# A tile's three products as three passes over its row blocks instead of three products per block

## What is computed

```python
h = _rmsnorm(x, norm_w) * (1.0 + scale[:, None]) + shift[:, None]
proj = h @ w_in
q, k, v, ga, u, gp, z, xbc, dt_raw, gl = jnp.split(proj, ...)
ya = _sink_window_attention(q, k, v, rel_bias, sinks) * silu(ga)
yb = _multiscale_pool(u, pool_w, pool_scale) * silu(gp)
yc = _ssd_branch(z, xbc, dt_raw, ...)
g = sigmoid(gl).reshape(b, s, 3, D_MODEL)
merged = g[:, :, 0] * (ya @ w_pa) + g[:, :, 1] * (yb @ w_pb) + g[:, :, 2] * (yc @ w_pc)
return x + gate[:, None] * (merged @ w_out)
```

## Time and profile before

| | us |
|---|---|
| median of 3 runs (lowest to highest) | 1238.05 (1238.03 to 1238.07) |
| time of the profiled execution | 1237.72 |
| its span, first to last instruction | 1235.8 |
| PE busy in the span | 1155.9 (94%) |
| DVE busy | 602.1 (49%) |
| POOL busy | 532.4 (43%) |
| ACT busy | 513.1 (42%) |
| mean granted TensorE clock | 0.970 |

### The profile page before, as it was taken

The page is one execution under the profiler, slowest core; times in us unless marked ns, Lnnn a source line. Parts: engine busy times, 40 slices in busy tenths (PEclk is TensorE's granted clock), DMA queues, the critical chain, the costliest instruction groups (busy, mean ns, idle before and its releaser), DMA issues.

```text
span 1235.8 us, 14931 instructions
## 1 busy us (share of the span) xinstructions
PE 1155.9 (94%) x5906; PEld 952.6 (77%) x5906; DVE 602.1 (49%) x741; ACT 513.1 (42%) x880; POOL 532.4 (43%) x392
## 2 busy tenths in 40 slices
PE   3289999999999999999989999999999999999996
PEld 2278888887888887788767888888788887778875
DVE  6754115655878633322435222565778754132434
ACT  1234334675543543322334422765454443232332
POOL 1524443444433435554533443453343425454540
PEclk9569999999999999999998999999999999999998
DMA  9824552233444233333223553332534423333321
GB/s 353 281 67 127 182 154 69 73 99 94 127 121 115 74 86 90 104 96 102 86 71 94 143 182 95 86 86 69 147 81 131 112 76 84 103 103 102 86 85 68
DMA packets 211460, 139.18 MB, mean 113 GB/s; under 512 B 11416, under 2 KB 203968, under 8 KB 209344
## 3 DMA queue, kind: packets, MB, share of 16 engines
q1 hardware_dynamic: 209968, 133.52, 37.5%
q10 hardware_dynamic: 1424, 4.72, 1.1%
HBM read 135.08 MB, written 2.62 MB: 111 GB/s over the span
## 4 chain that ended last, share of the span: by engine, by line
PE 82%; DVE 6%; DMA 5%; POOL 3%; ACT 2%; SPq 2%; issue 1%; DVEq 0%; ACTq 0%; POOLq 0%
PE main L462 72%; DMA raw<-in_w_in 4%; PE psC L462 4%; PE psA L462 3%; POOL tmp L421 1%; DVE h_lo L1238 1%; POOL w_lo L429 1%; PE psB L462 1%; DMA icnt<-in_inv_count 1%; DVE xbc L1193 1%; DVE tmp L968 1%; ACT w_hi L725 1%; DVE y_lo L1233 1%; DVE zs L1269 1%; SPq L381 1%
## 5 line engine op out<-in xcount | busy, mean ns | idle before, releaser
L429 POOL TENSOR_TENSOR w_lo<-raw,w_hi 128x512 fp32r<-128x512 f32 x360 | 507.3, 1431 | 644.8 <-ACT w_hi L725 644.8
L462 PE MATMUL main<-h_hi,w_hi 128*128 128x512 f32 x1184 | 473.1, 400 | 14.9 <-DVE h_lo L1010 5.9
L462 PE MATMUL main<-h_hi,w_lo 128*128 128x512 f32 x1184 | 463.4, 391 | 0.0
L462 PE MATMUL main<-h_lo,w_hi 128*128 128x512 f32 x1184 | 463.1, 391 | 0.0
L725 ACT ACTIVATE w_hi<-raw 128x512 fp32r<-128x512 f32 x360 | 208.4, 623 | 383.8 <-PE main L462 303.3
L462 PEld LDWEIGHTS main<-h_hi,w_hi 128*128 128x128 f32 x1184 | 223.8, 189 | 73.3 <-issue 22.0
L462 PEld LDWEIGHTS main<-h_hi,w_lo 128*128 128x128 f32 x1184 | 223.5, 189 | 48.0
L462 PEld LDWEIGHTS main<-h_lo,w_hi 128*128 128x128 f32 x1184 | 224.1, 189 | 46.5 <-issue 1.9
L1227 DVE TENSOR_TENSOR tmp<-main,misc 128x512 f32<-128x512 f32 x32 | 22.1, 691 | 201.9 <-PE main L462 201.9
L1073 DVE SCALAR_TENSOR_TENSOR misc<-main,lcol,misc 128x511 f32<-128x511 f32 (+2 forms) x96 | 71.9, 749 | 65.4 <-ACT misc L725 62.8
L462 PE MATMUL main<-y_hi,w_hi 128*128 128x512 f32 x256 | 101.6, 397 | 1.4 <-DVE y_lo L1233 1.4
(11 more groups left out here) (189 smaller groups left out, 1017.9 us busy)
## 6 DMA issues: line engine op xcount, KB each, us to landing
raw<-in_w_in SPq DMA_DIRECT2D x132, 512.0 KB, 3.8
zs<-in_w_ada SPq DMA_DIRECT2D x8, 1024.0 KB, 7.9
big<-in_w_ada SPq DMA_DIRECT2D x8, 1024.0 KB, 8.9
xbc<-in_w_ada SPq DMA_DIRECT2D x16, 512.0 KB, 4.8
raw<-in_w_pc SPq DMA_DIRECT2D x16, 512.0 KB, 3.7
raw<-in_w_out SPq DMA_DIRECT2D x16, 512.0 KB, 3.7
tmp<-step_rows SPq DMA_DIRECT2D x8, 512.0 KB, 4.2
big<-step_rows SPq DMA_DIRECT2D x8, 512.0 KB, 5.1
```

The costliest lines, as they stand in the source:

```text
L429: nc.gpsimd.tensor_tensor(w_lo[:, b, k:k + BT_, :], raw[:, b, k:k + BT_, :], w_hi[:, b, k:k + BT_, :].bitcast(F32), ALU.subtract).then_inc ...
L462: return nc.tensor.matmul(o, a, b_, start=start, stop=stop)
```

## The change

`tile` makes three loops of the one. The first does high by high for all blocks, and waits ahead of blocks 0 and 4 for the high half alone (`s_hi[b]`, ACT's). The second does high by low (`w_hi` with the low moving operand) for all blocks. The third does low by high, and waits ahead of blocks 0 and 4 for `s_split[b]`. With `ready`, the first pass waits for `s_mh` of each block and the second for `ready` of each block. The number of matmuls and their operands are the same. ACT, DVE, POOL and SP issue the same instructions in the same order, with the same waits.

```diff
--- before.py
+++ after.py
@@ -466,11 +466,17 @@
                 pe.wait_ge(s_evac[b], l * COUPLES + u)
                 for k in range(kt):
                     if k % BT_ == 0:
-                        pe.wait_ge(s_split[b], (l * COUPLES + u) * 2 + (k + BT_) * 2 // kt)
+                        pe.wait_ge(s_hi[b], (l * COUPLES + u) * 2 + (k + BT_) * 2 // kt)
+                    if ready is not None:
+                        pe.wait_ge(s_mh, l * KT + k + 1)
+                    mm(main[b][:, :], w_hi[:, b, k, :], rhs_hi[:, k0 + k, :], k == 0, False)
+                for k in range(kt):
                     if ready is not None:
                         pe.wait_ge(ready, l * KT + k + 1)
-                    mm(main[b][:, :], w_hi[:, b, k, :], rhs_hi[:, k0 + k, :], k == 0, False)
                     mm(main[b][:, :], w_hi[:, b, k, :], rhs_lo[:, k0 + k, :], False, False)
+                for k in range(kt):
+                    if k % BT_ == 0:
+                        pe.wait_ge(s_split[b], (l * COUPLES + u) * 2 + (k + BT_) * 2 // kt)
                     last = mm(main[b][:, :], w_lo[:, b, k, :], rhs_hi[:, k0 + k, :], False, k == kt - 1)
                 last.then_inc(s_tile[b], 1)
```

## The result

| | before | after |
|---|---|---|
| median of 17 runs each (lowest to highest), us | 1238.03 (1235.24 to 1239.94) | 1239.88 (1237.97 to 1241.21) |
| ratio, with its 95% interval | | 1.0015 (1.0008 to 1.0022) |
| time of the profiled execution, us | 1237.72 | 1238.16 |
| its span, us | 1235.8 | 1236.2 |
| mean granted TensorE clock | 0.970 | 0.966 |

The changed kernel is slower by 0.15%, 1.9 us, with an interval of 1.0 to 2.7 us. By the bound of 0.2% (2.5 us) that is no change, though the interval reaches just beyond the bound. The forecast was 1238.2 us in a range of 1234.8 to 1241.2. The three runs of before that were shown ahead of the prediction lay within 0.04 us, while 17 runs lie within 4.7 us: single executions say little here about 2 us, and what follows goes by the inside of the traces and by ratios of many runs.

What follows compares the result with a forecast made beforehand. PE, busy 94% of the span, was taken as the bound, so only its waits counted. Terms -3.8 - 0.3 - 2.5 + 5.0 + 1.8 = +0.2 us on the median 1238.05 gave 1238.2 us, range 1234.8 to 1241.2.

Steps and rivals of the forecast that it cites:

- the likeliest case: The forecast itself, chance 0.48: 1238.2 us, running from 1236.5 to 1239.5 by the bounds of the clock.
- Mixing steps 1 to 3: First tile of each step no longer waits for POOL's split: gain of 1.9 us a layer, 3.8 in all.
- Step 0: First mixing step: the gain becomes a wait of `states` for DVE, 0 in layer 0, 0.3 us in layer 1.
- `U_B`: Turns from a `w_pb` tile to the gate tile lose their stall: 14 x 0.18 = 2.5 us gained.
- The order in `U_OUT`: First `U_OUT` tile: PE waits for block 7's high part with 17 matmuls left, losing 2.5 us a layer, 5.0 in all.
- The clock: Clock falls after the roughly 5 us gap in `U_OUT`: 0.9 us lost a layer, bounds 0 and 1.5, together 1.8.
- the lower row: Profile stretch with dense work used to size the clock's loss: 1.77 us at 0.54, losing 0.8 us.
- The upper row: Profile stretch with dense work taken as the clock's upper bound: 3.11 us at 0.51, losing 1.5 us.
- the high clock: Rival: the clock stays high in the new `U_OUT` gap, 1236.4 us, still no change; chance 0.20.
- the clock low throughout: Rival: clock stays low through the `U_OUT` tile, 3.9 us lost per layer, 1244.2 us, slower; chance 0.15.
- step 0: Rival: DVE's chain moves with PE and step 0 keeps its gain; with clock high 1234.1 us, faster; chance 0.12.
- the `U_B` turns that gain nothing: Rival: another wait ends at the same moment in `U_B`, so 2.5 us are missing, 1240.7 us, slower; chance 0.05.

Runs made afterwards that it cites:

- e5: The changed kernel plus 20 matmuls with unread results, filling PE's idle time before block 7 in the first `U_OUT` tile; 1237.44 us, ratio 0.9986.
- e2: The kernel before, with only the first `U_OUT` tile in three passes; 1247.37 us, ratio 1.0078.
- e11: The kernel before, unchanged, profiled a second further time; 1237.84 us in that profile.
- e3: The kernel before, with only the tiles of `U_B` in three passes; 1236.68 us, ratio 0.9986.
- e1: The changed kernel with the old order kept in the first `U_OUT` tile; 1232.75 us, ratio 0.9954.
- e4: The kernel before, with only the tiles of `U_MIX` in three passes; 1235.39 us, ratio 0.9981.
- e8: The changed kernel with DVE's last merge moved earlier and the second and third pass of the first `U_OUT` tile swapped; 1229.18 us, ratio 0.9916.
- e10: The kernel before, unchanged, profiled once more; 1241.14 us in that profile.

## Why the prediction was right

The range held, and so did the call of no change by the bound that it set. A slowdown clear of the noise is there, 1.9 us where 0.2 was forecast, and 1239.88 lies just above the 1239.5 at which the likeliest case by itself was to end. Each place did what was said of it, but for the size of the clock's loss. Term by term, in the profiled execution:

- **Mixing steps 1 to 3**: 3.8 us forecast. The lead of PE over the first profile grew from 309.44 - 307.75 = 1.69 us at `states` of step 0 to 410.08 - 406.72 = 3.36 behind the last such tile, 1.7 us; in layer 1 from 0 to 2.0. Measured 3.7. Step 1 in layer 0 gave 0.3 and not 0.54, for the PSUM read.
- **Step 0**: 0.3 forecast, about 0.4 seen, with the waits for DVE in its place as forecast.
- **`U_B`**: 2.5 forecast. The lead grew from 3.36 to 507.21 - 502.20 = 5.01 us in layer 0 and by the same in layer 1; less what the last turn gives back, 3.1. The turn was worth 0.22 us and not 0.18: some starts behind a restart are 0.01 us wide too, which I left out.
- **The order in `U_OUT`**: 5.0 forecast, 4.9 measured by e5.
- **The clock**: 1.8 forecast, 3.6 measured, in the trace and by e5. This is the term that was mis-sized. The step that failed is "I take 0.9, near the lower row, because part of the low time lies in the idle time". In layer 0 the clock was low from inside the gap (595.1) to 601.9 us, 12.85 - 10.73 = 2.1 us lost, over my upper bound of 1.5: the low stretch was 6.8 us long and 4.7 of it met work, where my two rows were 3.1 and 1.8 us long; in layer 1 it fell only when PE restarted, nearly the whole low stretch met work, and 12.24 - 10.73 = 1.5 us were lost. In e2 it was 2.8 and 1.3. The upper row was no bound, but the usual case. The warning of the Trainium skill ("TensorE: Matmul & The Clock Gate", section "Why this matters for your kernels") against idle gaps between bursts held here in each of the six tiles seen with the gap of 4.95 us.

With what was measured the sum is -3.7 - 0.4 - 3.1 + 4.9 + 3.6 = +1.3 us, inside the interval of 1.0 to 2.7. That my forecast for the sum came so near owes something to luck: 1.8 us too little for the clock, 0.7 too little for the gains.

The two profiled executions themselves lie only 0.4 us apart, not 1.3, and the rest lies at places that are in no term. The changed kernel's was 1.57 us ahead at 205 us already (the same matmul starts at 205.05 before and 203.48 after), and e11, the kernel before once more, is as far ahead there (203.54). Between the layers the changed kernel's execution lost 0.6 us.

Of the rivals, the high clock and the clock low throughout are refuted by e5 and the traces, step 0 by its wait for DVE, and the `U_B` turns that gain nothing by e3. What I had left out is that the clock also falls, now and then, behind the old order's gaps; I had read from one profile that they leave it alone. In e1, e3 and e4 it fell at six of six tiles, against two of six in the unchanged kernel. Seven of these eight falls cost 1.35 to 1.7 us of lead, one in e1 2.9. Whether the change of the arrival time does that or chance is open. The gains of e1, e3 and e4 (5.7, 1.7 and 2.4 us, where their places show 7.2, 3.1 and about 4) came short in the timed runs by 1.4 to 1.7 us. An estimate from the counts gives about as much (two falls per execution against two in three executions, at 1.5 us each, are 2.0 us), but that this is the cause isn't shown.

## What to carry to other kernels

Splitting a wait in two moves what each needs ahead or back, and the price stands where the operand that comes last is now asked for first: check each call of a shared helper for what arrives late there, and let that call have its own order. Ask of the engine that makes the late operand what stands ahead of it in its queue; here moving one merge and asking for low parts last turned a loss of 1.9 us into a gain of 10.4. A gap in PE is priced with the clock behind it: filling it with work that nobody reads tells the two apart. And look for the clock's loss behind the place too, not only in it.

## What the runs showed that I had not expected

- DVE's sum of the merge (L1235, the old L1229) took 1.75 to 1.77 us beside POOL's split and 0.69 us without it, and the low parts of the merged sum 7.71 us for seven, where block 7's, with POOL idle, took 0.69. One half of POOL's split took 1.28 to 1.30 us where it started ahead of DVE's work and 1.72 to 1.76 where it started beside it. The two engines slow each other there. It moved my estimate for e8 by 0.7 us.
- One gap of 4.95 us cost 1.3 to 2.8 us of lost pace behind it, and gaps of 0.53 and 1.75 us with 0.7 us of work between were enough for a fall in some executions, at 1.35 us of lead or more.
- The same kernel's executions spread over 3 to 6 us, with three in a row 0.04 us apart. The profiles of the kernel before (first, e10, e11) differ at four kinds of place: up to 1.6 us by 205 us, 0.5 in mixing step 1, 1.2 between the layers, and 1.35 to 1.6 behind the first `U_OUT` tile.
